# A state-space recurrence in four-token steps inside a two-block fp32 transformer kernel

## What is computed

```python
ab = exp(lam * dt)                      # complex, one per state (ab_re, ab_im)
bb = (ab - 1) / lam * b                 # k * b
bu = einsum('blgh,gph->blgp', u, bb)    # input to the states
s  = scan(s[t] = ab * s[t-1] + bu[t])   # over 256 tokens
y  = einsum('blgp,ghp->blgh', s_re, c_re) - einsum('blgp,ghp->blgh', s_im, c_im)
y  = y + d * xin
g  = gelu(y)
out = g * sigmoid(g @ w_glu + b_glu)
```

## Time and profile before

| what | value |
|---|---|
| median of 3 runs | 2969.25 us (2968.87 to 2969.46) |
| the profiled execution | 2969.18 us |
| its span, first to last instruction | 2967.5 us |
| TensorE busy | 2950.7 us, 99% |
| VectorE busy | 2013.8 us, 68% |
| ScalarE busy | 1731.3 us, 58% |
| POOL busy | 494.0 us, 17% |
| granted TensorE clock | 0.999 of full speed |

### The profile page before, as it was taken

The page is one execution under the profiler, slowest core; times in us unless marked ns, Lnnn a source line. Parts: engine busy times, 40 slices in busy tenths (PEclk is TensorE's granted clock), DMA queues, the critical chain, the costliest instruction groups (busy, mean ns, idle before and its releaser), DMA issues.

```text
span 2967.5 us, 37386 instructions
## 1 busy us (share of the span) xinstructions
PE 2950.7 (99%) x13302; PEld 2428.2 (82%) x13302; DVE 2013.8 (68%) x2104; ACT 1731.3 (58%) x2454; POOL 494.0 (17%) x422
## 2 busy tenths in 40 slices
...
GB/s 257 182 160 197 198 201 193 201 184 197 194 194 220 191 224 205 208 221 185 268 186 188 186 177 179 215 208 210 205 203 185 200 195 193 192 192 194 192 191 162
DMA packets 298844, 588.43 MB, mean 198 GB/s; under 512 B 18464, under 2 KB 18480, under 8 KB 298352
## 3 DMA queue, kind: packets, MB, share of 16 engines
...
...
## 4 chain that ended last, share of the span: by engine, by line
PE 93%; DVE 3%; issue 1%; ACT 1%; DMA 1%; POOL 0%; SPq 0%; DVEq 0%; ACTq 0%; POOLq 0%
PE banks L1729 93%; DVE wlo L1115 1%; DMA raw<-in_w_in 1%; DVE W L1526 0%; ACT whi L610 0%; PE banks L1732 0%; DVE W L1518 0%; DVE banks L1519 0%; DVE banks L1521 0%; ACT L610 0%; ACT G L610 0%; ACT W L610 0%; DVE W L1386 0%; POOL G L516 0%; DVE banks L1520 0%
## 5 line engine op out<-in xcount | busy, mean ns | idle before, releaser
L1115 DVE TENSOR_TENSOR wlo<-raw,whi 128x1024 fp32r<-128x1024 f32 x1047 | 1391.9, 1334 | 863.9 <-ACT whi L610 857.0
L610 ACT ACTIVATE whi<-raw 128x1024 fp32r<-128x1024 f32 (+1 forms) x1049 | 1106.9, 1059 | 1047.5 <-PE banks L1729 937.8
L1729 PE MATMUL banks<-whi,Y 128*128 128x512 f32 x4800 | 1484.4, 389 | 0.3 <-DVE W L1214 0.2
L1729 PEld LDWEIGHTS banks<-whi,Y 128*128 128x128 f32 x4800 | 901.0, 188 | 188.1 <-issue 0.9
L1729 PE MATMUL banks<-wlo,Y 128*128 128x512 f32 x2400 | 933.7, 389 | 0.0
L1729 PE MATMUL banks<-whi,XH 128*128 128x512 f32 x1792 | 706.3, 394 | 7.4 <-DVE wlo L1115 6.9
L1729 PE MATMUL banks<-whi,XL 128*128 128x512 f32 x1792 | 698.1, 390 | 0.0
L1729 PE MATMUL banks<-wlo,XH 128*128 128x512 f32 x1792 | 698.0, 389 | 0.0
L1729 PEld LDWEIGHTS banks<-wlo,Y 128*128 128x128 f32 x2400 | 450.6, 188 | 93.2
L1729 PEld LDWEIGHTS banks<-whi,XH 128*128 128x128 f32 x1792 | 336.5, 188 | 87.0 <-issue 10.6
L1729 PEld LDWEIGHTS banks<-whi,XL 128*128 128x128 f32 x1792 | 336.4, 188 | 71.1
(11 more groups left out here) (256 smaller groups left out, 1187.9 us busy)
## 6 DMA issues: line engine op xcount, KB each, us to landing
raw<-in_w_in SPq DMA_DIRECT2D x383, 512.0 KB, 4.0
raw<-in_w_mlp_up SPq DMA_DIRECT2D x128, 512.0 KB, 3.9
raw<-in_w_mlp_down SPq DMA_DIRECT2D x128, 512.0 KB, 3.8
raw<-in_w_mlp_in SPq DMA_DIRECT2D x128, 512.0 KB, 3.8
raw<-in_w_mlp_out SPq DMA_DIRECT2D x128, 512.0 KB, 3.7
raw<-in_w_branch SPq DMA_DIRECT2D x80, 512.0 KB, 4.6
raw<-in_w_out SPq DMA_DIRECT2D x64, 512.0 KB, 4.3
...
```

The lines of the kernel that those rows point to most:

```text
L610: return nc.scalar.activation(out_, in_, f, **kw)
L1115: tt(wlo[:, i % RING, :], raw[:, i % RING, :], whi[:, i % RING, :].bitcast(F32), ALU.subtract)\
L1729: return nc.tensor.matmul(out_, l, r, start=start, stop=stop, **kw)
```

## The change

The state is kept only for every fourth token. Token 4q + k is phase k of step q. The 32 channels of a tile times four phases make 128 rows of one stacked input `U` (64 steps); the stacked input weights are B times the powers 3 to 0 of the transition, and the scan runs over 64 steps with the fourth power. The output of the four phases is C times the powers 1 to 4 of the state before, plus a direct product of the stacked input with C x power x B, a block lower-triangular 128 x 128 matrix per tile (`RE`), with d on its diagonal. Four tiles make a batch: 8 batches, nine units apart, from position 24.

- TensorE: `s5_in` has 8 matmuls of 64 columns per batch, `s5_out` 12 of 63 or 64 columns per batch (4 direct, 8 from states), all with 128 x 128 weights. New are `s5_rows` (two transposes at 125 of the first block) and `s5_direct` (64 matmuls at -7, 32 weight columns and 128 moving columns, in four column tiles).
- POOL: `s5_prepare` takes the place of `make_tables`: a table of 64 steps for each tile, products of powers with B rows, C times k times powers, with 112 transfers through DRAM. The last part starts at chunk 12, unit 4 of the feed-forward part. The states have a quarter of the instructions.
- SyncE loads for each batch 512 KB of input weights, 512 KB of state output weights, a 384 KB table and four pieces of the direct matrix.
- VectorE: `s5` for 8 batches; `skip` is gone; the powers in `s5_params` and a new `s5_direct` (at -5) are added.
- ScalarE: `token_move`, 16 copies after batch 3 (positions 60 to 63) and 16 after batch 7 (96 to 99), undo the phases; each batch's bank is copied to `YRAW`; the GELU moves to 100. The moves of the S5 projection are as many as before and now follow the VectorE transpose.
- The last feed-forward chunk of block 1 and the direct product wait for all preparation transfers.

The core of the diff (indentation cut):

```diff
+S5_TILES, S5_BATCHES, PH = 32, 8, 4
+TQ = T // PH
+BATCH = 4 * TQ
+U = slot(W, 2, 2).rearrange("p (j q) -> p j q", q=TQ)
...
+PREP_DMAS = 1 + 3 + S5_BATCHES * 9 + 2 + 2 * S5_BATCHES + 2 * S5_BATCHES + 2
+RB = [slot(Z, 2 + i) for i in range(2)]
+RW = [slot(Z, 8 + i) for i in range(2)]
+RE = [G[:, 512 * i:512 * i + 512].rearrange("p (e c) -> p e c", e=4) for i in range(2)]
+TAB = [G[:, SL + 768 * i:SL + 768 * i + 768].rearrange("p (r t) -> p r t", r=3) for i in range(2)]
+TAB_DMAS = 7
...
-S5Q, S5D, HQ2, HD2, GQ = 26, 5, 70, 5, 110
-S5_TILES = 32
+S5Q, S5D, S5L, HQ2, HD2, GQ = 24, 9, 6, 70, 5, 110
...
+def phase_move(m, h, src):
+    tq, k = m // PH, m % PH
+    return (U[B * k:B * k + B, 16 * h:16 * h + 16, :].rearrange("p j (t w a) -> p w t j a", t=NT, w=4)[:, tq],
+            src[B * tq:B * tq + B].rearrange("p (t j a k) -> p k t j a", t=NT, j=16, k=PH)[:, k])
+def token_move(m, h):
+    k, e = m // 4, m % 4
+    return (GS[B * e:B * e + B, 4 * h:4 * h + 4, :].rearrange("p i (q k) -> p k i q", k=PH)[:, k],
+            YRAW[B * k:B * k + B].rearrange("p (i e q) -> p e i q", i=4, e=4)[:, e])
...
-for j in range(S5_TILES):
-    yield S5Q + S5D * (j // 2) - (0 if j % 2 else 3) if j >= NTAB else 6 + j
-    if j == 0:
-        sp_.wait_ge(S("tables_saved"), 32 * S5_TILES // TG)
-    if j >= NTAB:
-        sp_.wait_ge(S("s5_state_ready"), j - NTAB + 1)
-    sp_.dma_start(TAB[j % NTAB], A["tables"][j]).then_inc(S(f"table_in{j % NTAB}"), 16)
+yield 2
+sp_.wait_ge(S("e_out"), 1)
+sp_.dma_start(A["es"].rearrange("i p c -> p i c"), ESB).then_inc(S("es_saved"), 16)
+for i in range(S5_BATCHES):
+    yield 8 + 3 * i if i < 2 else S5Q + S5D * (i - 2) + S5L + 5
+    if i == 0:
+        sp_.wait_ge(S("es_saved"), 16)
+        sp_.wait_ge(S("prep_dma"), 16 * PREP_DMAS)
+    if i >= 2:
+        sp_.wait_ge(S("s5_read"), i - 1)
+    landed = S(f"table_in{i % 2}")
+    sp_.dma_start(RB[i % 2], A["bst"][i]).then_inc(landed, 16)
+    sp_.dma_start(TAB[i % 2], A["tables"][i]).then_inc(landed, 16)
+    sp_.dma_start(RW[i % 2], A["wst"][i]).then_inc(landed, 16)
+    for k in range(PH):
+        sp_.dma_start(RE[i % 2][B * k:B * k + B, :, B * k:P],
+                      A["es"][i].rearrange("(e h) c -> h e c", e=4)[:, :, 0:P - B * k]).then_inc(landed, 16)
...
+for i in range(S5_BATCHES):
+    r, state = ROT[i % 2], STATE[i % 2]
+    c, s = (TAB[i % 2][:, k].unsqueeze(1).to_broadcast([P, 2, BATCH]) for k in range(2))
+    pool.wait_ge(S("s5_r_ready"), i + 1)
+    if i >= 2:
+        pool.wait_ge(S("s5_read"), i - 1)
     tt(state, r, c, ALU.mult)
...
+def s5_prepare():
...
+pool.wait_ge(used, mlp_base(1, 1) + 4)
+pool.wait_ge(S("s5_params_by_act"), 5)
+pool.wait_ge(S("s5_params_by_dve"), 6)
+dma(A["pow"].rearrange("r k j s -> (k j) r s"), ROWS.rearrange("p (r s) -> p r s", r=2))
...
+for g in range(S5_BATCHES):
+    pool.wait_ge(used, mlp_base(1, 4 + g // 2) + 4 + 8 * (g % 2))
+    for k in range(PH):
+        part = slice(B * k, B * k + B)
+        dma(POWB[part], A["pow"][:, PH - 1 - k, 4 * g:4 * g + 4, :].rearrange("r j s -> r (j s)").partition_broadcast(B))
+        dma(BROW[part], A["b_rows"][:, :, 4 * g:4 * g + 4, :].rearrange("h r j s -> h r (j s)"))
+    all_landed()
...
+    dma(A["bst"][g], BOUT)
+for i in range(2):
+    dma(CRAW[i], A["c_t"][i])
+all_landed()
+wst = A["wst"].rearrange("g p r j k c -> r k p g j c")
+for g in range(S5_BATCHES):
+    pool.wait_ge(used, mlp_base(1, 8 + g // 2) + 4 + 8 * (g % 2))
...
+    tt(t1, ci, knim, ALU.mult)
+    tt(t2, ci, knre, ALU.mult)
+    tt(CW[0][:, js], cr, kre, ALU.mult)
+    chain(tt(CW[1][:, js], cr, knim, ALU.mult))
+    tt(CW[0][:, js], CW[0][:, js], t1, ALU.add)
+    chain(tt(CW[1][:, js], CW[1][:, js], t2, ALU.add))
+    for x in range(2):
+        dma(A["wst"][g, :, x, :, 0:PH - 1, :], CW[x][:, js, 1:PH, :])
+pool.wait_ge(used, mlp_base(1, 12) + 4)
...
+tt(CW4[0], CRAW[0], kre, ALU.mult)
+chain(tt(CW4[1], CRAW[0], knim, ALU.mult))
+tt(CW4[0], CW4[0], t1, ALU.add)
+chain(tt(CW4[1], CW4[1], t2, ALU.add))
+for x in range(2):
+    for g in range(S5_BATCHES):
+        dma(A["wst"][g, :, x, :, PH - 1, :], CW4[x][:, 4 * g:4 * g + 4])
+chain(nc.gpsimd.memset(G[:, 0:SL], 0.0))
+for i in range(2):
+    dma(BST[i], A["b_states"][i])
+assert issued[0] == PREP_DMAS
+all_landed()
...
+if (b, ph, i) == (2, "a", 0):
+    act.wait_ge(S("e_mm"), 1)
...
+if ch[0] == "s5":
+    for i in range(8):
+        yield p + 1 + i
+        if i == 0:
+            act.wait_ge(S("stage_turned2"), n + 1)
+        for m in range(2 * i, 2 * i + 2):
+            ins = a(*phase_move(m, ch[1], MB2[n % 2]))
+    ins.then_inc(S("stage_moved2"), 1)
+    continue
...
-yield S5Q + 87
-act.wait_ge(S("s5_y"), 8)
+for i in range(S5_BATCHES):
+    at = S5Q + S5D * i + S5L + 2
+    yield at
+    act.wait_ge(S("s5_read"), i + 1)
+    a(YRAW[:, BATCH * (i % 4):BATCH * (i % 4) + BATCH], PT[1][:, 0:BATCH]).then_inc(S("s5_y"), 1)
+    if i % 4 == 3:
+        for m in range(16):
+            if m % 4 == 0:
+                yield at + 1 + m // 4
+                act.wait_ge(S("s5_y"), i + 1)
+            ins = a(*token_move(m, i // 4))
+        ins.then_inc(S("s5_turned"), 1)
+yield at + 5
+act.wait_ge(S("s5_turned"), 2)
 a(GS, GS, ACT.Gelu_apprx_tanh).then_inc(S("s5_g"), 1)
 for h in range(2):
-    yield S5Q + 88 + h
+    yield at + 6 + h
...
+def s5_direct():
+    yield -5
+    dve.wait_ge(S("e_mm"), 1)
+    for e in range(4):
+        part = slice(B * e, B * e + B)
+        ins = nc.vector.tensor_copy(DIAG[part], ident[part, B * e:B * e + B])
+    chain(ins)
+    for h in range(2):
+        acc = PU[h].rearrange("p (i c) -> p i c", i=4)
+        for i in range(4):
+            stt(ESB[:, 4 * h + i, 0:B], DIAG, s5_d[:, 4 * h + i:4 * h + i + 1], acc[:, i, 0:B], ALU.mult, ALU.add)
+        ins = nc.vector.tensor_copy(ESB[:, 4 * h:4 * h + 4, B:P], acc[:, :, B:P])
+    ins.then_inc(S("e_out"), 1)
...
 def s5():
-    for j in range(32):
-        if j % 4 == 2 and j > 2:
-            yield S5Q + S5D * (j // 2) + 1
-            skip(j // 4 - 1)
-        yield S5Q + S5D * (j // 2) + 3 + j % 2
-        c, s = (TAB[j % NTAB][:, i].unsqueeze(1).to_broadcast([P, 2, T]) for i in range(2))
-        bu = PU[j % 2].rearrange("p (r t) -> p r t", r=2)
-        dve.wait_ge(S("bu_mm"), j + 1)
-        dve.wait_ge(S(f"table_in{j % NTAB}"), 16 * (j // NTAB + 1))
+    for i in range(S5_BATCHES):
+        yield S5Q + S5D * i + 2
+        c, s = (TAB[i % 2][:, k].unsqueeze(1).to_broadcast([P, 2, BATCH]) for k in range(2))
+        m = TAB[i % 2][:, 2]
+        bu = pairs_of(PU[i % 2])
+        dve.wait_ge(S("bu_mm"), i + 1)
+        dve.wait_ge(S(f"table_in{i % 2}"), 16 * TAB_DMAS * (i // 2 + 1))
         tt(D2, bu, s, ALU.mult)
         chain(tt(bu, bu, c, ALU.mult))
         tt(bu[:, 0], bu[:, 0], D2[:, 1], ALU.add)
         chain(tt(bu[:, 1], bu[:, 1], D2[:, 0], ALU.subtract))
-        if j >= 2:
-            dve.wait_ge(S("s5_state_ready"), j - 1)
-        m = mag[:, j:j + 1].to_broadcast([P, T])
-        nc.vector.tensor_tensor_scan(ROT[j % 2][:, 0], m, bu[:, 0], 0.0, ALU.mult, ALU.add)
-        nc.vector.tensor_tensor_scan(ROT[j % 2][:, 1], m, bu[:, 1], 0.0, ALU.mult, ALU.add).then_inc(S("s5_r_ready"), 1)
-        dve.wait_ge(S("s5_r_ready"), j + 1)
-    yield S5Q + 86
-    skip(7)
-def skip(i):
-    dve.wait_ge(S("s5_read"), 4 * i + 4)
-    stt(GS[:, i, :], XI[:, i, :], s5_d[:, i:i + 1], PT[1][:, 0:T], ALU.mult, ALU.add).then_inc(S("s5_y"), 1)
+        yield S5Q + S5D * i + 3
+        if i >= 2:
+            dve.wait_ge(S("s5_state_ready"), i - 1)
+        nc.vector.tensor_tensor_scan(ROT[i % 2][:, 0], m, bu[:, 0], 0.0, ALU.mult, ALU.add)
+        nc.vector.tensor_tensor_scan(ROT[i % 2][:, 1], m, bu[:, 1], 0.0, ALU.mult, ALU.add).then_inc(S("s5_r_ready"), 1)
+        dve.wait_ge(S("s5_r_ready"), i + 1)
...
+def s5_rows():
+    yield PARQ + 21
+    pe.wait_ge(S("s5_params_by_dve"), 5)
+    for r in range(2):
+        ins = tr(PU[0][:, P * r:P * r + P], POW[:, r, 0:4].rearrange("p k j -> p (k j)"))
+    ins.then_inc(S("s5_rows_mm"), 1)
+def s5_direct():
+    yield -7
+    pe.wait_ge(S("prep_dma"), 16 * PREP_DMAS)
+    for i in range(8):
+        for r in range(2):
+            for e in range(4):
+                c, j = B * e, 4 * i + e
+                ins = mm(PU[i // 4][c:c + B, P * (i % 4):P * (i % 4) + P], BST[r][:, j, :],
+                         CW[r][:, j].rearrange("p k c -> p (k c)"), start=r == 0, stop=r == 1,
+                         tile_position=(0, c), skip_group_check=True)
+    ins.then_inc(S("e_mm"), 1)
 def s5_in():
-    for m in range(16):
-        yield S5Q + S5D * m
-        i, c0 = m // 2, 64 * (m % 2)
-        if m == 0:
-            pe.wait_ge(S("s5_b_in"), 32)
-            pe.wait_ge(S("stage_turned2"), 1)
-        else:
-            if m == 8:
-                pe.wait_ge(S("stage_turned2"), 2)
-            pe.wait_ge(S("s5_r_ready"), 2 * m)
+    for i in range(S5_BATCHES):
+        yield S5Q + S5D * i
```

(80 more changed lines are left out.)

189 lines of the change are left out of this document (105 added, 84 removed).

## The result

The changed kernel takes 3016.9 us (median of five executions), the kernel before 2969.3 us on the same chip: a ratio of 1.016, 95% interval 1.0145 to 1.0172. A sixth execution took 13345.7 us and is left out; no profile shows why it was so slow. Forecast were 2979.2 us and at most 2989. The profiled execution takes 3013.44 us, 44.3 us more than the one of before.

What follows compares the result with a forecast made beforehand. TensorE, busy 99% of the span, was taken as the bound. Groups +5.0, direct product +3.9, rows +0.3, boundary wait +3.0, unit 99 wait +4.8, gain -7.0 made +10.0 us on 2969.18: 2979.2 us, range 2966 to 2989.

Steps and rivals of the forecast that it cites:

- S5 groups, +5.0: TensorE's recurrence: input groups of 1.78 us and output groups of 2.68 us, 35.7 us against 30.7 us, +5.0 us.
- rivals 2 and 3: Group records at column pace, 0.056 us each (2962.7 us, chance 0.09); or half hidden, 0.08 us (2969.8 us, chance 0.06).
- Direct product +3.9: TensorE after unit -7: the new product block of 64 matmuls costs 3.9 us, bounds 3.5 and 7.2 us.
- the boundary's wait +3.0: Block boundary: TensorE's first transpose pair waits for VectorE's residual add behind `s5_direct`, +3.0 us, bounds 2 and 4.5.
- The wait at unit 99, +4.8: TensorE waits for ScalarE, whose list now holds token moves and the GELU: +4.8 us, bounds 0 and 8.
- The gain, -7.0: Recurrence: with 8 batches and no skip products on VectorE, TensorE's seven waits end, -7.0 us.
- At no cost: POOL's preparation in the feed-forward part and SyncE's loads in the recurrence were expected to add nothing.
- The cover of `raw`, 3.6 us: Recurrence: behind a batch's 1.45 MB on SyncE, `raw` is split at 14.5 and needed at 18.1, 3.6 us to spare.
- Rival 4: SyncE, recurrence: `raw` lands 5.6 us later behind table bursts, 2 us for each of six batches; 2991 us, chance 0.10.
- rival 5: POOL's preparation ends late, its last part taking over 120 us; at 131 us the kernel takes 2990 us; chance 0.08.

Runs made afterwards that it cites:

- experiment 2: The changed kernel without POOL's six products for seven of the eight groups, all loads and stores kept: 2992.5 us, ratio 1.0081.
- 8 to 13: Kernel before with skip products moved, table loads later or issued by POOL, or second tiles later: 2974.1, 2969.1, 2969.1, 2973.8, 2968.7, 2966.7 us.
- experiment 6: The changed kernel with the same preparation spread: a group's loads two at a time, the previous group's products between them: 2989.3 us, ratio 1.0070.

## Why the prediction was wrong, step by step

**S5 groups, +5.0: held, 0.9 short.** The input group in the changed kernel, from start to start, 1599.88 - 1598.17 = 1.71 us plus 0.12 for the slower matmul start after it; from unit to unit it is 1.83 us (forecast 1.78), the output group 2.73 (2.68): 36.5 us, where the old groups, counted the same way, take 30.6. That is 0.11 us a record; rivals 2 and 3 are out. So are, for such a record, the 81 ns of the Trainium skill's page "TensorE: Matmul & The Clock Gate", section Back-to-back issue gap.

```profile
1598.17 1.89 PE L1890 MATMUL banks<-W,Z 128*128 128x64 f32 x16
1599.88 0.48 PE L1890 MATMUL banks<-whi,XH 128*128 128x512 f32 x1
```

**Direct product +3.9 and the boundary's wait +3.0: right.** 3.8 and 2.9 us.

```profile
1444.91 0.39 PE L1890 MATMUL banks<-whi,Y 128*128 128x512 f32 x1
1445.23 3.70 PE L1890 MATMUL banks<-XF,W 128*32 128x128 f32 x128
1448.86 0.50 PE L1890 MATMUL banks<-whi,Y 128*128 128x512 f32 x1
...
1454.56 0.66 PE L1893 MATMUL banks<-identR,W 128*128 128x128 f32 x4 [2.69 <-DVE W L1822]
```

**The wait at unit 99, +4.8: right cause, wrong size.** It is 8.7 us. The mis-sized term is the token move: I took 0.41 us from a block move, and four take 2.66 us, 0.66 each; 16 x 0.25 = 4.0 us more. Counted from the end of unit 93 (1772.2), the scores of head 6 start at 33.5 us, where I had 29.5.

```profile
1785.48 2.67 ACT L699 ACTIVATE W<-W 32x256 f32<-32x256 f32 x4
1788.16 0.49 ACT L699 ACTIVATE W<-banks 128x384 f32<-128x384 f32 x1
...
1791.67 0.52 ACT L699 ACTIVATE WR<-W 128x384 fp32r<-128x384 f32 x1 [0.62 <-DVE W L1702]
```

TensorE stops earlier than I said, at head 5's triangular sums (1.93 us for VectorE's split behind that row) and then for `wlo` (0.7 and 2.2 us), not at the next scores. At unit 64, behind the first half's moves, 1.1 us are lost, which I had at nothing. The moves take ScalarE's lead there, but a split of 2.38 us on VectorE is needed as well: in experiment 2 the moves are the same, that split takes 1.23 us, and nothing is lost.

**The gain, -7.0: right, 7.4 at the seven units, about 8 in the whole stretch.** All seven waits are gone. Why they were there I had wrong in part (8 to 13): the pair of tiles on VectorE has a share, the skip product alone does not make them, and the rest is open.

**"At no cost", the step that failed: +28.3 us.** The prediction put the preparation at nothing since "POOL is busy 188 us with 206 in the same stretch today, and TensorE has no wait there". The 206 is a number of instructions, set against the 112 + 139 new ones; their busy time was not worked out. It makes POOL busy 299.6 us from 743 to 1410, for 188.0 before. And a sum over the whole part asks neither how many bytes go at once nor what is late when they do: experiment 6 keeps POOL as busy (287.6 us) and loses 3.7 us. The cover of `raw`, 3.6 us, I worked out for the tables of block 2, where loads can be late without harm (no wait there), and never for POOL's 64 loads in the feed-forward part, where `raw` comes 1.4 to 3.1 us later in the median, POOL makes VectorE's split longer at the same time, and ScalarE, with 2.6 us of work in a unit of 2.72 ahead of the residual add, cannot catch up. Rival 4 was the right mechanism at the wrong place; rival 5 did not happen: nothing waited for the preparation's end. With +28.3 put in, and 8.7 and 1.1 for ScalarE's waits, the sum is +43.3 us, for 44.3 in the profiled execution. The 28.3 is from that same trace, so this shows that nothing large is missing, not that such a term could have been forecast to the microsecond.
